# A hybrid encoder with routed experts: results added onto x, a comparison tournament for the experts, and filler products on TensorE

## What is computed

```python
for l in range(DEPTH):
    m = mixing_sublayer(x, ...)
    x = layer_norm(DN_ALPHA * x + m, ln_mix_g[l], ln_mix_b[l])
    f = moe_ffn(x, w_router, router_bias, exp_w_gate[l], exp_w_up[l], exp_w_down[l])
    x = layer_norm(DN_ALPHA * x + f, ln_ffn_g[l], ln_ffn_b[l])

def group_limited_router(x2d, w_router, router_bias):
    scores = jax.nn.softmax(x2d @ w_router, axis=-1)
    sel = scores + router_bias                       # 16 experts in 4 groups of 4
    sel_g = sel.reshape(n, N_GROUPS, EXPERTS_PER_GROUP)
    best = jnp.argmax(jnp.sum(lax.top_k(sel_g, 2)[0], axis=-1), axis=-1)
    masked = jnp.where(in_group(best), sel_g, -jnp.inf)
    _, idx = lax.top_k(masked, 2)                    # two experts, both of the best group
    wts = take(scores, idx) / sum
    return one_hot(idx) * wts                        # gates

def moe_ffn(...):
    for e in range(N_EXPERTS):
        y = y + gates[:, e] * ((silu(x @ w_gate[e]) * (x @ w_up[e])) @ w_down[e])
```

## Time and profile before

| | |
|---|---|
| median of 3 runs | 1052.97 us (1052.52 to 1054.11) |
| the profiled execution's own time | 1053.41 us |
| its span, first to last instruction | 1051.6 us |
| PE busy | 979.3 us (93%) |
| DVE / ACT / POOL busy | 793.9 / 654.9 / 525.5 us |
| mean granted TensorE clock | 0.966 of full speed |
| chain that ended last | PE 77%, DVE 19%, ACT 1%, issue 2%, DMA 0% |
| DMA | 268.53 MB, mean 255 GB/s |

### The profile page before, as it was taken

One profiled execution on the slowest core, in us unless ns is written; L12 is line 12 of the kernel. 1 busy time (PEld: TensorE's weight loads), 2 busy tenths in 40 slices (PEclk: granted clock), 3 DMA queues, 4 the chain that ended last, 5 costly groups with the idle time before them and its releaser, 6 DMA issues.

```text
span 1051.6 us, 15474 instructions
## 1 busy us (share of the span) xinstructions
PE 979.3 (93%) x4852; PEld 790.6 (75%) x4852; DVE 793.9 (75%) x967; ACT 654.9 (62%) x737; POOL 525.5 (50%) x285
## 2 busy tenths in 40 slices
PE   7999898599999999999999998995999999999995
PEld 5777777478788888877778777774888888888882
DVE  5996646788777777777878967477877787777776
ACT  5326623478788787777533357233878787878861
POOL 1631374266565656445425323741565665656563
PEclk9999899699999999999999998995999999999998
DMA  9615293399999999995813211934999999999962
GB/s 294 211 73 210 83 336 125 131 354 369 347 353 359 341 337 337 363 349 169 251 57 120 81 49 41 333 117 139 349 373 370 346 362 370 349 359 335 367 220 86
DMA packets 122307, 268.53 MB, mean 255 GB/s; under 512 B 10523, under 2 KB 26043, under 8 KB 121760
## 3 DMA queue, kind: packets, MB, share of 16 engines
q1 hardware_dynamic: 111136, 247.14, 64.8%
q0 software_dynamic: 11136, 20.96, 7.6%
HBM read 259.19 MB, written 27.79 MB: 273 GB/s over the span
## 4 chain that ended last, share of the span: by engine, by line
PE 77%; DVE 19%; issue 2%; ACT 1%; DVEq 0%; DMA 0%; SPq 0%; ACTq 0%
PE bank L782 34%; PE bank L800 18%; PE bank L437 14%; DVE bank L1179 7%; PE bank L760 2%; PE bank L583 2%; PE bank L754 1%; DVE moemem L1435 1%; DVE xTl L1148 1%; DVE w_gate L1155 1%; PE bank L835 1%; PE bank L831 1%; PE bank L603 1%; DVE w_gate L1156 1%; DVE w_down L1154 1%
## 5 line engine op out<-in xcount | busy, mean ns | idle before, releaser
L1682 POOL TENSOR_TENSOR wl<-w_down,wh 128x2048 fp32r<-128x2048 f32 x33 | 153.5, 4651 | 144.3 <-ACT wh L1047 144.3
L1148 DVE TENSOR_TENSOR wl<-w_gate,wh 128x2048 fp32r<-128x2048 f32 (+1 forms) x75 | 166.7, 2222 | 54.2 <-ACT wh L1047 35.5
L1148 DVE TENSOR_TENSOR wl<-w_up,wh 128x2048 fp32r<-128x2048 f32 x66 | 151.1, 2293 | 28.7 <-ACT wh L1047 27.4
L1047 ACT ACTIVATE wh<-w_down 128x2048 fp32r<-128x2048 f32 x66 | 126.8, 1920 | 28.5 <-PE bank L782 27.6
L1047 ACT ACTIVATE wh<-w_up 128x2048 fp32r<-128x2048 f32 x66 | 126.6, 1918 | 27.6 <-PE bank L800 21.7
L782 PE MATMUL bank<-wh,xTh 128*128 128x512 f32 x528 | 143.2, 393 | 0.2 <-ACT wh L1047 0.2
L782 PE MATMUL bank<-wl,xTh 128*128 128x512 f32 x528 | 142.5, 392 | 0.4 <-DVE wl L1148 0.4
L782 PE MATMUL bank<-wh,xTl 128*128 128x512 f32 x528 | 142.4, 392 | 0.0
L1614 POOL TENSOR_TENSOR wl<-w_gate,wh 128x2048 fp32r<-128x2048 f32 x16 | 73.5, 4594 | 125.2 <-ACT wh L899 98.2
L1047 ACT ACTIVATE wh<-w_gate 128x2048 fp32r<-128x2048 f32 x66 | 126.5, 1917 | 12.8 <-PE bank L800 6.4
L1148 DVE TENSOR_TENSOR xTl<-bank,xTh 128x512 fp32r<-128x512 f32 (+1 forms) x168 | 90.0, 574 | 41.3 <-issue 16.9
(11 more groups left out here) (228 smaller groups left out, 1767.6 us busy)
## 6 DMA issues: line engine op xcount, KB each, us to landing
w_up<-in_exp_w_up SPq DMA_DIRECT2D x32, 2048.0 KB, 20.1
w_down<-in_exp_w_down SPq DMA_DIRECT2D x32, 2048.0 KB, 18.7
w_gate<-in_exp_w_gate SPq DMA_DIRECT2D x32, 2048.0 KB, 18.9
w_gate<-in_w_in SPq DMA_DIRECT2D x13, 1024.0 KB, 5.6
w_gate<-in_w_out SPq DMA_DIRECT2D x8, 1024.0 KB, 5.1
y_rows<-moemem SPq DMA_DIRECT2D x8, 512.0 KB, 10.5
x_rows<-xtok POOLq DMA_DIRECT2D x8, 512.0 KB, 3.0
w_up<-y_rows SPq DMA_DIRECT2D x8, 512.0 KB, 5.0
```

The source lines that it names most:

```text
L1047: act.activation(wh[s][:, :], slot[r][p][:, cols], ACT.Copy).then_inc(half_high, 1)
L1148: return dve.tensor_tensor(out, src, high.bitcast(F32), ALU.subtract)
L1682: pool.tensor_tensor(wl[s][:, :], slot[r][p][:, cols], wh[s][:, :].bitcast(F32), ALU.subtract)\
```

## The change

There are four edits.

- **x as the start of the sums.** `zero_choices` goes. In each layer, behind the load of expert 0's gate weights, SP now stores the four tiles of `xtok` into `yd` (`fill_choices`), and POOL waits for these stores before its chunk loop. The gates are divided by ALPHA, and the epsilon of the second normalisation by ALPHA squared, so that the normalised result is the same. `join` goes.
- **The last chunk in two fp32r parts.** ACT writes the high part of the last result (`last_result`), DVE the low part (`last_low_part`), and PE adds each with fp32r products. PE copies `ycomb` instead of xtok, in the order written in `add_choices`.
- **In-group comparisons.** The two `first_max` searches and the mask go. Six comparisons of shifted pieces of a group of four write a 4 x 4 table per group, a sum over it gives each expert's number of losses, and `selb` is (losses < 2) times (own group is the best). The logit halves are added by PE, in the product that replaces the transpose.
- **Filler products.** `idle_products(24)` ahead of the wait for `selb`, `idle_products(16)` behind the product for the first tokens. They write a part of bank 7 that nobody reads.

```diff
@@ -348,12 +350,10 @@
             sp.dma_start(ycomb[j], yd[l][P * j:P * j + P, :]).then_inc(y_in[j], 16)
-    def zero_choices():
-        sp.wait_ge(pool_chain, 1)
-        for l in range(DEPTH):
-            for r in range(TT):
-                sp.dma_start(yd[l][P * r:P * r + P, :], xg).then_inc(y_zeroed, 16)
+    def fill_choices(l):
+        for j in range(TT):
+            sp.dma_start(yd[l][P * j:P * j + P, :], xtok[:, j, :]).then_inc(y_filled, 16)
@@ -381,8 +381,6 @@
             load_piece(l, q)
-            if q == 9 and l == 0:
-                zero_choices()
@@ -406,6 +404,7 @@
         load_expert(l, 0, 0, 0)
+        fill_choices(l)
@@ -710,12 +709,13 @@
             pe.wait_ge(lgT_set, TT * l + j + 1)
-            mm = pe.transpose(bank[2][:, 2 * E * j:2 * E * j + 2 * E], lgT[:, P * j:P * j + P],
-                              ident[0:2 * E, 0:2 * E])
+            mm = pe.matmul(bank[2][:, E * j:E * j + E], lgT[:, P * j:P * j + P],
+                           cst[0:2 * E, K_SUM:K_SUM + E], start=True, stop=True)
+        idle_products(24)
@@ -731,6 +731,7 @@
         mm.then_inc(first_done, 1)
+        idle_products(16)
@@ -746,6 +747,11 @@
         mm.then_inc(late_done, 1)
+    def idle_products(n):
+        for _ in range(n):
+            pe.matmul(bank[7][:, 0:256], wrs[:, 0:4, :], wrs[:, :, :], start=True, stop=True)
@@ -824,17 +830,37 @@
         narrow(l, c, 5)
-    def add_choices(l, j, end):
-        pe.wait_ge(xc_set, TT * l + j + 1)
-        for h in range(2):
-            pe.matmul(bank[2 * j + h][:, :], ident, xtok[:, j, 512 * h:512 * h + 512], start=True, stop=False)
-        pe.wait_ge(last_set, l + 1)
-        pe.wait_ge(y_set, end + (l + 1))
-        for h in range(2):
-            mm = pe.matmul(bank[2 * j + h][:, :], last_hot[:, P * j:P * j + P], ysb[:, 512 * h:512 * h + 512],
-                           start=False, stop=True)
-        mm.then_inc(y_added, 1)
+    def add_choices(l, end):
+        def whole(j, h):
+            if h == 0:
+                pe.wait_ge(y_in[j], 16 * (l + 1))
+            pe.matmul(bank[2 * j + h][:, :], ident, ycomb[j][:, 512 * h:512 * h + 512], start=True, stop=False)
+        def chosen(j, part):
+            if j == 0 and part == 0:
+                pe.wait_ge(last_set, l + 1)
+                pe.wait_ge(y_set, end + (l + 1))
+            if j == 0 and part == 1:
+                pe.wait_ge(yl_set, l + 1)
+            for h in range(2):
+                mm = pe.matmul(bank[2 * j + h][:, :], last_hot[:, P * j:P * j + P],
+                               y_parts[part][:, 512 * h:512 * h + 512], start=False, stop=(part == 1))
+            return mm
+        whole(0, 0)
+        whole(0, 1)
+        chosen(0, 0)
+        whole(1, 0)
+        chosen(0, 1).then_inc(y_added, 1)
+        whole(1, 1)
+        chosen(1, 0)
+        chosen(1, 1).then_inc(y_added, 1)
+        for j in range(2, TT):
+            for h in range(2):
+                whole(j, h)
+            chosen(j, 0)
+            chosen(j, 1).then_inc(y_added, 1)
@@ -874,8 +900,7 @@
         end = first_chunk(pe, l, E)
-        for j in range(TT):
-            add_choices(l, j, end)
+        add_choices(l, end)
@@ -1038,6 +1063,14 @@
         act.activation(ysb[:, 512:1024], bank[6][:, :], ACT.Copy, scale=gate_cur[:, :]).then_inc(y_set, 1)
+    def last_result(c, l):
+        act.wait_ge(half_used, halves_done(c, 2, 1))
+        act.wait_ge(cur_set, c + (l + 1))
+        for n in range(2):
+            x = act.activation(y_parts[0][:, 512 * n:512 * n + 512], bank[5 + n][:, :], ACT.Copy, scale=gate_cur[:, :])
+        x.then_inc(y_set, 1)
@@ -1113,7 +1146,7 @@
             piece(l + 1, 1)
-        result(end, l, 1)
+        last_result(end, l)
@@ -1263,7 +1296,8 @@
             link(dve.bn_aggr(mv[:, 2 * j:2 * j + 2], bnm[j]))
-        link(dve.tensor_scalar(ve[:, j:j + 1], mv[:, 2 * j + 1:2 * j + 2], EPS, None, ALU.add))
+        link(dve.tensor_scalar(ve[:, j:j + 1], mv[:, 2 * j + 1:2 * j + 2],
+                               EPS / ALPHA ** 2 if ffn else EPS, None, ALU.add))
@@ -1282,11 +1316,14 @@
                                  ALU.mult, ALU.add).then_inc(row_set[j] if ffn else ln_out, 1)
-    def join(l, j):
-        dve.wait_ge(y_in[j], 16 * (l + 1))
-        dve.scalar_tensor_tensor(xtok[:, j, :], xtok[:, j, :], ALPHA, ycomb[j], ALU.mult, ALU.add)\
-           .then_inc(xc_set, 1)
+    def last_low_part(l, c):
+        dve.wait_ge(y_set, c + (l + 1))
+        for n in range(2):
+            cols = slice(512 * n, 512 * n + 512)
+            x = dve.scalar_tensor_tensor(y_parts[1][:, cols], bank[5 + n][:, :], gate_cur[:, :],
+                                         y_parts[0][:, cols].bitcast(F32), ALU.mult, ALU.subtract)
+        x.then_inc(yl_set, 1)
@@ -1325,12 +1362,12 @@
     def route(l):
+        link(dve.memset(scr[:, 1920:2176], 0.0))
-        ps = bank[2][:, 0:2 * TT * E].rearrange("p (j h e) -> p j e h", j=TT, h=2)
+        ps = bank[2][:, 0:TT * E].rearrange("p (j e) -> p j e", j=TT)
-        link(dve.tensor_reduce(lg, ps, AX.X, ALU.add))
-        link(dve.tensor_reduce(top, lg, AX.X, ALU.max))
-        link(dve.tensor_tensor(lg, lg, bc3(top, E), ALU.subtract))
+        link(dve.tensor_reduce(top, ps, AX.X, ALU.max))
+        link(dve.tensor_tensor(lg, ps, bc3(top, E), ALU.subtract))
@@ -1341,32 +1378,25 @@
         dve.tensor_tensor(pr[:, :, 3:5], s4[:, :, 0:2], s4[:, :, 2:4], ALU.add)
-        link(dve.tensor_tensor(pr[:, :, 5:6], s4[:, :, 0:1], s4[:, :, 3:4], ALU.add))
+        dve.tensor_tensor(pr[:, :, 5:6], s4[:, :, 0:1], s4[:, :, 3:4], ALU.add)
+        for d in range(1, EG):
+            near, far = s4[:, :, 0:EG - d], s4[:, :, d:EG]
+            dve.tensor_tensor(beat[:, :, EG * d:EG * EG:EG + 1], near, far, ALU.is_ge)
+            x = dve.tensor_tensor(beat[:, :, d:d + (EG + 1) * (EG - 1 - d) + 1:EG + 1], far, near, ALU.is_gt)
+        link(x)
+        dve.tensor_reduce(lose.rearrange("p j e -> p (j e)"),
+                          beat.rearrange("p g (e f) -> p (g e) f", f=EG), AX.X, ALU.add)
-        def first_max(hot, vals, keys, width, m):
-            link(dve.tensor_reduce(m, vals, AX.X, ALU.max))
-            link(dve.tensor_tensor(hot, vals, bc3(m, width), ALU.is_equal))
-            kb = keys.unsqueeze(1).broadcast_to([P, TT, width])
-            link(dve.tensor_tensor(hot, hot, kb, ALU.mult))
-            link(dve.tensor_reduce(m, hot, AX.X, ALU.max))
-            link(dve.tensor_tensor(hot, hot, bc3(m, width), ALU.is_equal))
-        link(dve.tensor_tensor(gkey, gkey, bc3(m1, G), ALU.subtract))
-        gb = gkey.rearrange("p j g -> p (j g)").unsqueeze(2).broadcast_to([P, TT * G, EG])
-        s4m = smk.rearrange("p j (g m) -> p (j g) m", g=G)
-        link(dve.scalar_tensor_tensor(s4m, gb, 1e30, s4, ALU.mult, ALU.add))
-        ke = cst[:, K_KE:K_KE + E]
-        first_max(oh1, smk, ke, E, m1)
-        link(dve.scalar_tensor_tensor(smk, oh1, -3e38, smk, ALU.mult, ALU.add))
-        first_max(oh2, smk, ke, E, m2)
-        link(dve.tensor_tensor(selb[:, :, :], oh1, oh2, ALU.add))
+        link(dve.tensor_tensor(gkey, gkey, bc3(m1, G), ALU.is_equal))
+        own = gkey.rearrange("p j g -> p (j g)").unsqueeze(2).broadcast_to([P, TT * G, EG])
+        by_group = [x.rearrange("p j (g m) -> p (j g) m", g=G) for x in (lose, selb[:, :, :], oh1, oh2)]
+        link(dve.scalar_tensor_tensor(by_group[1], by_group[0], 2.0, own, ALU.is_lt, ALU.mult))
@@ -1374,7 +1404,9 @@
         dve.tensor_scalar(away, selb[:, :, 0], 1.0, 1000.0, ALU.subtract, ALU.mult)
-        link(dve.memset(zero16, 0.0))
+        dve.memset(zero16, 0.0)
+        dve.scalar_tensor_tensor(by_group[2], by_group[0], 1.0, own, ALU.is_lt, ALU.mult)
+        link(dve.scalar_tensor_tensor(by_group[3], by_group[0], 1.0, own, ALU.is_equal, ALU.mult))
@@ -1416,8 +1448,8 @@
         link(dve.reciprocal(m1, m1))
-        dve.tensor_tensor(gt[:, 0:TT], gt[:, 0:TT], m1, ALU.mult)
-        link(dve.tensor_tensor(gt[:, TT:2 * TT], gt[:, TT:2 * TT], m1, ALU.mult))
+        dve.scalar_tensor_tensor(gt[:, 0:TT], gt[:, 0:TT], 1.0 / ALPHA, m1, ALU.mult, ALU.mult)
+        link(dve.scalar_tensor_tensor(gt[:, TT:2 * TT], gt[:, TT:2 * TT], 1.0 / ALPHA, m1, ALU.mult, ALU.mult))
@@ -1579,11 +1611,9 @@
         hot_last(l)
-        join(l, 0)
-        for j in range(1, TT):
-            join(l, j)
+        last_low_part(l, end)
@@ -1730,8 +1760,6 @@
         pool.wait_ge(x1_stored, 16 * TT * (l + 1))
-        if l == 0:
-            pool.wait_ge(y_zeroed, 16 * TT * DEPTH)
@@ -1742,6 +1770,7 @@
             pool.wait_ge(late_set, l + 1)
+            pool.wait_ge(y_filled, 16 * TT * (l + 1))
@@ -1755,7 +1784,7 @@
     c[:, K_IOTA:K_IOTA + P] = p[None, :]
-    c[:, K_KE:K_KE + E] = E - np.arange(E)
+    c[0:2 * E, K_SUM:K_SUM + E] = np.tile(np.eye(E), (2, 1))
```

More of the change, by code:

```diff
@@ L58 @@
 NCOL = 106
-K_ID, K_IOTA, K_KE, K_KG, K_TOK = 0, 128, 256, 272, 276
+K_ID, K_IOTA, K_SUM, K_KG, K_TOK = 0, 128, 256, 272, 276
 NCONST = 284
@@ L159, in build @@
```

(8 more changed lines are left out.)

## The result

| | before | changed |
|---|---|---|
| median of 4 runs each, on one chip | 1053.12 us (1052.52 to 1054.11) | 1046.76 us (1044.84 to 1047.53) |
| the profiled execution's own time | 1053.41 us | 1044.84 us |
| its span | 1051.6 us | 1042.9 us |
| mean granted clock | 0.966 | 0.973 |
| PE / DVE busy | 979.3 / 793.9 us | 984.5 / 784.0 us |

The medians lie 6.4 us apart. The ratio of the runs is 0.9933, interval [0.9916, 0.9949]: 7.1 us faster, between 5.4 and 8.8. The profiled execution is the fastest of the four of the changed kernel, so its 8.57 us of gain are more than a median run shows.

What follows compares the result with a forecast made beforehand. PE was taken to bound the chunks, DVE's short dependent steps the routing. Choice 4.8, clock 2.4 and layer 0's end 2.0, less 0.5 for fills, gave 8.7 us off 1053.41, 1044.7; from the median 1044.3, range 1040.5 to 1049.

Steps and rivals of the forecast that it cites:

- No clock: Rival: in both routings filler fails, the clock falls as before and slow products hold L738 up; 1047.7 us, 16%.
- DVE's choice, both layers: Routing: comparisons replace DVE's dependent search steps, 2.4 us earlier in each layer, 4.8 in both.
- sum of the halves on PE, and the memset: Routing: logit sum moves into PE's product and the memset lies in DVE's wait; both cost nothing.
- clock: Both routings: filler keeps PE's clock up part of the time; between 0 and 4.7 us, middle taken, 2.4.
- end of layer 0: Layer 0's end: faster fp32r groups let POOL's shift end sooner, first turn 2.0 us earlier; bounds 1.0 and 3.2.
- fills: Routing: storing x behind expert 0's gate load may delay the last x1d store; 0.25 us a layer, 0.5 lost in all.
- end of layer 1: Layer 1's end: gains nothing, since the first group comes after 3.48 us of PE instead of 3.44.
- Full clock: Rival: filler keeps 2.4 GHz through both routings, so the whole 4.7 us comes back; 11.0 gained, 1042.0 us, 17%.
- The filler's price: Routing: at half clock filler could hold the ranks up by 1.4 us and L738 by 0.6; nothing was taken.
- Late rows: Rival: in each routing the last x1d store or the gather ends with the fills, 2.2 us late; 1048.2 us, 15%.
- Slower: Rival: the first gather queues behind slow fills, rows 6.4 us late in each layer; 3.6 slower, 1057.0 us, 4%.
- Lost in the loads: Rival: DMA alone sets layer 0's last chunks, so its routing's 3.4 us gain dies there; 1047.7 us, 4%.

Runs made afterwards that it cites:

- e6: Kernel before with only the in-group comparisons added, halves still summed on DVE: 1050.31 us, ratio 0.9962.
- e3: Changed kernel with the four logit transposes and DVE's sum of the halves back in place of PE's sum product: 1046.46 us, ratio 0.9935.
- e1: Changed kernel without its 40 filler products: 1048.19 us, ratio 0.9958 to the kernel before.
- e7: Kernel before with only x stored into the sums, the last result in two parts and no join: 1052.33 us, ratio 0.998.
- e2: Changed kernel with zero stores back in layer 0's mixing and no stores of x, so other data in layer 1: 1050.64 us.
- e4: Changed kernel with denser filler, 36 and 26 products instead of 24 and 16, plus 6 and 8 in smaller holes: 1044.68 us, ratio 0.9931.
- e8: Changed kernel with the denser filler (36, 6, 26 and 8 products), measured a second time: 1044.63 us, ratio 0.9921.
- e5: Changed kernel with transposes and DVE's sum of the halves back, and the denser filler (36, 6, 26, 8): 1045.75 us, ratio 0.9914.
- e10: Kernel before with filler products alone (54, 6, 26 and 8): 1051.83 us, ratio 0.9989.

## Why the prediction was right, and which terms were not

The time, 1046.8 against a forecast of 1044.3, lies in the stated range of 1040.5 to 1049. It is just outside the forecast's own 1042.5 to 1046.5, and nearer to the 1047.7 of "No clock"; the traces and not the time tell these two apart. The gain lies where it was put. That the profiled execution's 1044.84 meets the sum's 1044.7 is luck, by the 1.9 us of the late chunks. The sum of 8.7 was too large by about two:

| term | predicted | shown | by |
|---|---|---|---|
| DVE's choice, both layers | 4.8 | 4.9 to `selb` (6.82 - 4.36 and 6.81 - 4.37) | the traces; e6 has 4.6 of it at the chunk with the addition of the halves left on DVE |
| sum of the halves on PE, and the memset | nothing | cost 0.9 (0.39 + 0.07 a layer) | 1.75 against 1.29 us from the last product of the logits to the first table, in both layers; e3 |
| clock | 2.4 | 0.4 to 1.4 by the filler | e1 against three profiles of the changed kernel |
| end of layer 0 | 2.0 | 1.5 | 23.5 against 25.0 in every profile with the edit; e7 |
| fills | -0.5 | 0 | e2 in layer 0; POOL's wait in both layers |
| end of layer 1 | nothing | 0.07 | the traces |

With the shown terms the sum is 4.9 - 0.9 + (0.4 to 1.4) + 1.5 = 5.9 to 6.9; the ratios of its three measurements say 6.0 to 7.2. Against the kernel before instead of e1, what the routings gained beyond `selb` is 0.7 to 1.6: even without filler (e1) layer 1's was 0.25 shorter than `selb` explains; its third group of weight products took 1.38 and not 1.84 us.

**The choice.** The step held as worked out. First table to the end of `selb` was to be 7.06 - 2.44 = 4.62 us and was 4.36 + 0.22 = 4.58. (The 7.06 has 0.24 for an instruction whose row says 0.22.)

**The sum product.** This is the term that failed outright: "4 with 16 columns for 4 with 32: nothing" counted the columns and not what kind of operation it is. The records have eight products for the program's four, and on the chain each takes 1.00 / 8 = 0.125 us, with 16 columns, which is what a filler product of 256 columns takes (3.13 / 24 = 0.13). It was no visible loss only because the same edit spares DVE its first reduction, which the prediction had counted with the choice. The memset, which was to hide in DVE's wait, seems to have taken 0.07.

**The clock.** The forecast took the middle between nothing and all, and feared the holes behind each filler. The clock did fall, behind 1.74 us of nothing ahead of the ranks and 1.06 behind them; the second hole that it named, behind the second filler, was gone in layer 0, where the slow filler reached up to `L739`, and 0.86 us in layer 1. The mechanism is confirmed by e4: with more filler in all of these places the clock stays at 2.4 GHz through both routings and the routing is 1.7 us shorter a layer, 3.5 in both, inside the bounds of 0 to 4.7. Against the kernel before it is 3.8, so the ceiling of 4.7, 1.9 and 2.8, was too high, by its 2.8 for layer 1 above all (2.0). Such filler kept the clock in both routings of e4, in layer 0 of e8 and in layer 1 of e5, and not in the other routings; why is open. So "Full clock" is reached in one profile and not held.

The Trainium skill (TensorE: Matmul & The Clock Gate, HAM oscillation — how this bites in real kernels) puts a throttled PE down to long idle gaps between bursts of products. The gap of 7.20 us before agrees with it. The changed kernel's 0.59 and 0.56 behind gaps of 1.74 and 1.06 us do not fit it: keeping the idle gaps short was not enough here. The prediction read that the trace before "shows nothing for gaps of two". It did show one, at the end of layer 0, where the clock fell at 535.6, within a gap of 2.33 us:

```profile
535.82 0.58 PE L437 MATMUL bank<-xTh,wh 128*128 128x256 f32 x1 [2.33 <-DVE xTl L1148]
```

With this row holes of two us speak for a lower middle than 2.4. The term also varies from one execution to the next: the same kernel gave 0.9, 0.9 and 0.2 in layer 0.

**The filler's price.** Nothing was taken for it, and in the changed kernel nothing shows. The second filler of layer 0 ran at half clock for the most part and ended at 188.56 + 3.57 = 192.13. The chain goes over DVE there, whose table was done at 192.23, and `L739` started at 192.27:

```profile
191.53 0.70 DVE wh L1440
192.27 1.24 PE bank L739 x8
```

With the eight further products of the denser filler there is a price where they run at the low clock: the late tables start 1.0 us later in layer 1 of e8 than in e4.

**The end of layer 0.** The order was right: POOL's shift is what the turn waits for. The turn came 1.74 earlier instead of 2.0, since the first statistics came 3.73 and not 3.5 behind `narrow`; and the eight turns then took 1.11 us instead of 0.89, which gave back the rest.

**The fills.** "Late rows", 15%, is ruled out: the wait for the last row of x is 7.93, 7.97 and 8.02 us in layer 0 without fills, before, and with fills, and in layer 1 7.94, 9.19 and 8.12. (The 189.3 of the term's upper bound stands in no row; the wait before ended at 185.84.) The Trainium skill (DMA: Bandwidth & Descriptors, Queues, rings and completion order) has the engines take packets from their queues in turn, by which 2 MB more in SP's queue don't hold POOL's store; these numbers agree. "Slower" needed fills that last beyond 195; DMA was through by about 191. (Its 1057.0 is added to the profiled execution's time, the other rivals' to the median; 1056.6 would match them.) The 0.73 us for which e4's PE waited in layer 1 for gathered rows are not the fills': e10, without them, waited 0.97.

**Lost in the loads.** With the routing shorter by 3.4 us, the other 16 chunks of layer 0 did not take longer (293.5 us, and 295.4 and 295.9 in the repeats, against 295.4). So the gain was not given back there.

## What to carry to other kernels

A maximum search on DVE whose steps wait for each other can be turned into comparisons that don't: twelve dependent steps of some 0.25 us became six independent ones at 0.12 and a sum, and that gain arrived whole. Before an addition is moved into a product "for nothing", find a row of the same kind of product and compare how many the records show and how long each takes, not its columns. Filler products gave 1.7 us a routing where the clock stayed full, and 0.2 to 0.9 where holes were left; the rest changed from run to run. Filler in front of a product that something waits for has a risk: when the clock falls all the same it takes longer (2.06 us instead of 1.19 for eight) and makes that product late. So look for what the engine behind waits for, here the late tables, before filling the hole ahead of it.

## What the runs showed of the hardware

- Four products of fp32 data with 16 columns stand as eight in the records and take 1.06 us at the full clock, with granted clock 1.00 in the stretch; four transposes of fp32 with 32 columns take 0.67.
- The granted clock can fall in the midst of dense products: in layer 1 of the changed kernel PE had been busy from 712.48 on when it fell at 714.0, after waits of 1.68 and 1.06 us with small products between. In layer 0 it fell at 188.4, with PE busy from 187.99 on, was back at 191.8, and fell again at 195.2 in the wait ahead of `L747`. In layer 1 of e10 it fell at 727.1, and the longest wait of PE in that routing was 0.97 us. A low clock in a stretch is therefore not to be looked for in the work of that stretch alone.
- POOL waits 7.8 to 8.0 us for the last 512 KB that it stores beside a 2 MB load of SP in layer 0, and 7.9 to 9.3 in layer 1, whether or not 2 MB more stand behind that load.
- Executions of one kernel on one chip differ by up to 7.8 us (1042.73 to 1050.55 in e4), and between the profiles the late chunks of layer 0 and the mixing of layer 1 differ most, where there is no edit but the sum product. Effects of one or two us were read from stretches of the trace for that reason, and the medians used as a check.
